# Two column chunks in step: each weight pass of a tile run for one chunk, then the other, in two PSUM banks

## The chip, the cores and the metric

The kernel runs on one core of one Trainium2 chip. The metric is the device time of one execution in microseconds (us), as the median of several runs. A profiled execution of the same kernel gives the trace from which the rows below are read.

## The reference

Two small transformer blocks follow each other on one sequence of 512 tokens, width 1024, in float32. The first puts 16 meta tokens ahead (528 tokens in all) and has two layers: differential attention and a gated MLP with a causal convolution of width 3, then latent attention and the same MLP again. The second has a projection, a convolution branch and a windowed attention branch, gates, and a third MLP. Cut to what matters here:

```python
def conv_ffn(h, g_norm, w_in, conv_w, conv_b, w_out):
    xn = rms_norm(h, g_norm)
    a, b = jnp.split(xn @ w_in, 2, axis=-1)            # 1024 -> 2 x 2816
    ap = jnp.pad(a, ((0, 0), (CONV_W - 1, 0), (0, 0)))
    a_conv = conv_b
    for j in range(CONV_W):
        a_conv = a_conv + ap[:, j:j + L] * conv_w[j]
    return h + (jax.nn.silu(a_conv) * b) @ w_out       # 2816 -> 1024

h = concatenate([meta, x])                             # 528 tokens
h = diff_attn_layer(h, ...);  h = conv_ffn(h, ...)     # layer 0
k_nope, k_rope, v = shared_latent_kv(h, ...)
h = mla_layer(h, ...);        h = conv_ffn(h, ...)     # layer 1
x = rms_norm(h, final_norm)[:, 16:]                    # 512 tokens
return second_block(x, ...)
```

## The kernel before

Tokens lie along the free dimension and features along the 128 partitions, so an activation of width 1024 is 8 blocks of 128 rows. The weights come from HBM as one stream of "halves" of 128 x 1024 values (8 blocks of 128 x 128) through a ring of four buffers. ScalarE rounds a half to `w_hi` (fp32r, the form that TensorE multiplies in one pass), GpSimd writes the remainder to `w_lo`. Activations are held as such pairs too: `x_hi`, `x_lo` and `g_hi`, `g_lo`. A product of full precision is then three passes per block, hi x hi, hi x lo and lo x hi (`passes`, lines 789, 790, 791 of the kernel, in this order: `x_hi` with `w_hi`, `x_lo` with `w_hi`, `x_hi` with `w_lo`).

An output tile is 128 features by T tokens, and `tile` computes it on TensorE from one half of weights, with 8 blocks (6 in the last down projection of a layer's MLP). T is T1 = 528, T3 = 516 or T2 = 512. A PSUM bank holds 512 float32 columns, so `chunks(T)` gives one chunk for T2 and two chunks of T/2 columns for T1 (264) and T3 (258), in banks 2(j mod 2) and 2(j mod 2) + 1. Before the change a tile of two chunks runs all blocks for the first chunk, then all blocks for the second: 24 passes in one bank, 24 in the next. The next tile uses the other two banks. VectorE is released by `half_done` after the last pass of the tile, reads both banks in one instruction, and gives them back by `tile_taken`.

Within a tile, TensorE waits once for the weights (`lo_ready`) and for the bank pair (`tile_taken`), and before each block for the activation (`ready`, which is `x_ready` or `g_ready`). That last wait only stands in the first chunk.

Which two-chunk tiles go through `tile`, by the calls in the program: tiles 2 to 7 of the output projection of layer 0 (T1), the 44 up tiles of the first MLP (T1) and tiles 2 to 7 of its last down projection (T1, 6 blocks), three tiles of the query latent (T1), tiles 2 to 7 of the output projection of layer 1 (T3), and the 22 tiles at even places among the up tiles of the second MLP (T3; those at odd places are T2, one chunk). Tiles of one chunk, the paired first two tiles of a projection (`tile_pair`), the attention pieces and the down projections in `product` do not pass through the edited lines.

Of the kernel before, what the change touches and what calls it, by code (L numbers as in the profile page):

```python
# [32 lines left out]
P = 128  # L33
# [109 lines left out]
def ring(j):  # L143

    return (j + 2 * len([d for d in DOWNS.values() if d.j < j])) % 4
# [101 lines left out]
def program(nc, x_t, stream, params, positions, out):  # L247
    tabs_dram = nc.inline_tensor(rotary_tables(), "rotary_tables").ap()
    consts_dram = nc.inline_tensor(shape_constants(), "shape_constants").ap()
    with ExitStack() as ctx:  # L250
# [8 lines left out]
        w_hi = sb("w_hi", [P, 4, HW], F32R)  # L259
        w_lo = sb("w_lo", [P, 4, HW], F32R)  # L260
# [138 lines left out]
        ps = ctx.enter_context(nc.psum_tensor("ps", [P, 8, 512], F32))  # L399
# [141 lines left out]
        def chunks(T):  # L541

            return [(0, 0, T2)] if T == T2 else [(0, 0, T // 2), (1, T // 2, T // 2)]
# [241 lines left out]
        def _(pe):  # L785
            def passes(out_ap, j, b, xh, xl, k, cols, first, last):

                s, c = ring(j), slice(b * P, (b + 1) * P)
                nc.tensor.matmul(out_ap, w_hi[:, s, c], xh[:, k, cols], start=first, stop=False)  # L789
                nc.tensor.matmul(out_ap, w_hi[:, s, c], xl[:, k, cols], start=False, stop=False)  # L790
                return nc.tensor.matmul(out_ap, w_lo[:, s, c], xh[:, k, cols], start=False, stop=last)  # L791

            def tile(j, tl, blocks, xh, xl, T, ready, i=0, first=0):

                pe.wait_ge(lo_ready, j + 1 + 4 * i)
                wait(pe, tile_taken, tl - 1 - int(after_down(j)) + 4 * i)
                for bank, t0, n in chunks(T):
                    for b in range(blocks):
                        if ready and not bank:
                            pe.wait_ge(ready[0], ready[1] + b + 1)  # L800
                        last = passes(ps[:, 2 * (j % 2) + bank, 0:n], j, b, xh, xl, b,
                                      slice(first + t0, first + t0 + n), b == 0, b == blocks - 1)
                last.then_inc(half_done, 1)

            def pair_blocks(j, tl, m, n, blocks, xh, xl, T, ready, b0=0, b1=KD):
# [539 lines left out]
            for m in range(TILES_C):  # L1345
# [4 lines left out]
                if m == 3:  # L1350
                    pe.wait_ge(y_ready, 2)
                    for b in range(4):
                        last = nc.tensor.transpose(ps[:, 3, b * P:b * P + P], vt2[:, b * P:b * P + P], ident)
                    last.then_inc(vt2_done, 1)
                for u in range(8):
                    g, n = divmod(u, 4)
                    s_at = unit2_at(u)
                    k0 = 0 if n else P
                    if m == s_at + 2:
                        pe.wait_ge(p2_ready, u + 1)  # L1360
                        wait(pe, pt2_ready, u)
                        for i in range(4):
                            for kb in range(k0 // P, 2):
                                last = nc.tensor.transpose(ps[:, 6 + kb, i * P:i * P + P],
                                                           prob2[:, i, kb * P:kb * P + P], ident)
# [12 lines left out]
                for u in range(8):  # L1378
                    g, n = divmod(u, 4)
# [1439 lines left out]
```

## Time and profile before

| | |
|---|---|
| runs | 2045.72, 2044.54, 2044.59 us; median 2044.59 us |
| the profiled execution | 2045.36 us, span 2043.6 us |
| TensorE busy | 2020.7 us of the span, 13376 matmuls and as many weight loads |
| VectorE, ScalarE, GpSimd busy | 1322.9, 853.1, 1160.5 us |
| granted TensorE clock | mean 0.999 |
| bytes over DMA | 183.06 MB, mean 90 GB/s |

The busy time of TensorE counts the records of matmuls that overlap: a record lasts from the start of a pass to its modelled end, and the next pass starts well before that. The pace of the engine is therefore read from start to start.

### The profile page before, as it was taken

To read this page: it belongs to the slowest core of one execution; us is meant where nothing else is said; L and a number is where in the kernel's file an instruction comes from. 1 tells how busy PE (TensorE), PEld (TensorE's weight loads), DVE (VectorE), ACT (ScalarE), POOL (GpSimd) and SP (SyncE) were. 2 spreads that over 40 slices of the span, in tenths; PEclk is the share of its full clock that TensorE was granted. 3 is DMA by queue.
4 is the path that set the end of the run, shared out by engine and by line. 5 is a ranking of instruction groups with operands and counts; after the bars stand their busy time and mean duration, and the time that the engine had idled before them with its cause. 6 is when DMAs were issued, how large, how long until landed. Compare 5 with 4: busy or idle time off the path is not lost.

```text
span 2043.6 us, 37435 instructions
## 1 busy us (share of the span) xinstructions
PE 2020.7 (99%) x13376; PEld 1806.5 (88%) x13376; DVE 1322.9 (65%) x2193; ACT 853.1 (42%) x1493; POOL 1160.5 (57%) x1395
## 2 busy tenths in 40 slices
PE   9999999999999999999999999999999999999998
PEld 8889899999999988899998998777788888888987
DVE  7777757847746868856857768865512457857654
ACT  5444534432433477724432425344422234433433
POOL 6444356666657522146675767744445557666755
PEclk9999999999999999999999999999999999999999
DMA  5222122232233301122233233322223223232322
GB/s 188 75 73 81 53 83 93 78 114 89 88 108 104 104 32 43 32 89 93 71 118 100 87 99 103 112 80 78 82 93 99 87 83 102 84 113 83 124 83 83
DMA packets 51986, 183.06 MB, mean 90 GB/s; under 512 B 5648, under 2 KB 7824, under 8 KB 51856
## 3 DMA queue, kind: packets, MB, share of 16 engines
q1 hardware_dynamic: 50304, 178.87, 27.1%
q10 hardware_dynamic: 1552, 2.42, 0.3%
q8 instruction: 87, 1.43, 0.3%
q14 instruction: 43, 0.35, 0.1%
HBM read 179.17 MB, written 2.10 MB: 89 GB/s over the span
## 4 chain that ended last, share of the span: by engine, by line
PE 97%; DVE 2%; issue 1%; ACT 1%; DVEq 0%; ACTq 0%
PE ps L789 25%; PE ps L790 24%; PE ps L791 24%; PE ps L913 4%; PE ps L914 4%; PE ps L915 4%; PE ps L1162 2%; PE ps L1179 1%; PE ps L1072 1%; PE ps L1172 1%; PE ps L1103 1%; PE ps L1087 1%; PE ps L861 1%; PE ps L1173 0%; PE ps L1105 0%
## 5 line engine op out<-in xcount | busy, mean ns | idle before, releaser
L723 POOL TENSOR_TENSOR w_lo<-w_raw,w_hi 128x256 fp32r<-128x256 f32 x1140 | 962.6, 879 | 762.8 <-ACT w_hi L2219 742.0
L789 PE MATMUL ps<-x_hi,w_hi 128*128 128x264 f32 (+2 forms) x2504 | 823.1, 329 | 0.1
L790 PE MATMUL ps<-x_lo,w_hi 128*128 128x264 f32 (+2 forms) x2504 | 813.6, 325 | 0.0
L791 PE MATMUL ps<-x_hi,w_lo 128*128 128x264 f32 (+2 forms) x2504 | 812.3, 324 | 0.0
L789 PEld LDWEIGHTS ps<-x_hi,w_hi 128*128 128x128 f32 x2504 | 471.3, 188 | 49.9 <-issue 5.4
L790 PEld LDWEIGHTS ps<-x_lo,w_hi 128*128 128x128 f32 x2504 | 470.8, 188 | 42.1 <-issue 0.2
L791 PEld LDWEIGHTS ps<-x_hi,w_lo 128*128 128x128 f32 x2504 | 471.3, 188 | 39.6
L2219 ACT ACTIVATE w_hi<-w_raw 128x1024 fp32r<-128x1024 f32 x267 | 278.1, 1049 | 67.1 <-PE ps L791 51.4
L789 PE MATMUL ps<-g_hi,w_hi 128*128 128x264 f32 (+3 forms) x648 | 207.9, 321 | 1.0 <-DVE g_lo L1878 1.0
L790 PE MATMUL ps<-g_lo,w_hi 128*128 128x264 f32 (+3 forms) x648 | 205.9, 318 | 0.0
L791 PE MATMUL ps<-g_hi,w_lo 128*128 128x264 f32 (+3 forms) x648 | 205.6, 317 | 0.0
L2354 ACT ACTIVATE scratch<-scratch,par 128x512 f32<-128x512 f32 (+1 forms) x66 | 54.2, 821 | 342.3 <-DVE scratch L1603 342.3
L743 POOL TENSOR_TENSOR w_lo<-w_raw,w_hi 128x256 fp32r<-128x256 f32 x144 | 125.8, 902 | 75.6 <-ACT w_hi L2236 75.3
L789 PEld LDWEIGHTS ps<-g_hi,w_hi 128*128 128x128 f32 x648 | 121.9, 188 | 11.7 <-DVE g_lo L1878 1.4
L790 PEld LDWEIGHTS ps<-g_lo,w_hi 128*128 128x128 f32 x648 | 122.0, 188 | 9.2
L791 PEld LDWEIGHTS ps<-g_hi,w_lo 128*128 128x128 f32 x648 | 122.1, 188 | 8.7
L2153 DVE TENSOR_TENSOR scratch<-ps,acc 128x512 f32<-128x512 f32 x46 | 31.8, 691 | 120.3 <-PE ps L791 120.2
L914 PE MATMUL ps<-g_lo,w_hi 128*128 128x256 f32 (+1 forms) x384 | 108.4, 282 | 0.0
L915 PE MATMUL ps<-g_hi,w_lo 128*128 128x256 f32 (+1 forms) x384 | 108.0, 281 | 0.0
L913 PE MATMUL ps<-g_hi,w_hi 128*128 128x256 f32 (+1 forms) x384 | 107.9, 281 | 0.0
L1609 DVE SCALAR_TENSOR_TENSOR scratch<-scratch,par 128x512 f32<-128x512 f32 (+1 forms) x66 | 53.9, 817 | 71.3 <-ACT scratch L2354 71.3
L1617 DVE TENSOR_TENSOR scratch<-ps,r 128x512 f32<-128x512 f32 (+1 forms) x66 | 46.0, 696 | 77.6 <-PE ps L791 77.5
(278 smaller groups left out, 3052.8 us busy)
## 6 DMA issues: line engine op xcount, KB each, us to landing
w_raw<-stream SPq DMA_DIRECT2D x334, 512.0 KB, 3.5
h<-x_t SPq DMA_DIRECT2D x4, 528.0 KB, 6.9
out_t<-h SPq DMA_DIRECT2D x6, 256.0 KB, 2.3
scratch<-rotary_tables ACTq DMA_DIRECT2D x4, 264.0 KB, 5.3
out_t<-h ACTq DMA_DIRECT2D x2, 256.0 KB, 2.5
par<-params ACTq DMA_DIRECT2D x1, 342.0 KB, 4.9
scratch<-positions ACTq DMA_DIRECT2D x1, 256.0 KB, 2.6
cst<-shape_constants ACTq DMA_DIRECT2D x1, 193.0 KB, 6.0
```

What stands on the lines that cost most here:

```text
L723: last = nc.gpsimd.tensor_tensor(w_lo[:, ring(j), cols], w_raw[:, j % 4, cols], w_hi[:, ring(j), cols].bitcast(F32), ALU.subtract)
L743: last = nc.gpsimd.tensor_tensor(chunks_lo[:, slot, cols], src[:, cols], chunks_hi[:, slot, cols].bitcast(F32), ALU.subtract)
L789: nc.tensor.matmul(out_ap, w_hi[:, s, c], xh[:, k, cols], start=first, stop=False)
L790: nc.tensor.matmul(out_ap, w_hi[:, s, c], xl[:, k, cols], start=False, stop=False)
L791: return nc.tensor.matmul(out_ap, w_lo[:, s, c], xh[:, k, cols], start=False, stop=last)
L913: nc.tensor.matmul(out_ap, wh, xh, start=opens and q == 0, stop=False, skip_group_check=True)
L914: nc.tensor.matmul(out_ap, wh, xl, start=False, stop=False, skip_group_check=True)
L915: last = nc.tensor.matmul(out_ap, wl, xh, start=False, stop=q == 3, skip_group_check=True)
L1609: V.scalar_tensor_tensor(conv[:, 0:Tn], a_pad[:, c0 + 1:c0 + 1 + Tn], tap(1), conv[:, 0:Tn], ALU.mult, ALU.add).then_inc(conv_step, 1)
L1617: V.tensor_tensor(cut(b_val[:, 0:Tn], Tn), result(j + 1, Tn), cut(r[:, c0:T], Tn), ALU.mult).then_inc(tile_taken, 1)
L2219: A.activation(w_hi[:, ring(j), :], w_raw[:, j % 4, :], ACT.Copy).then_inc(hi_ready, 1)
L2354: A.activation(conv[:, 0:Tn], a_pad[:, T - Tn:T], ACT.Identity, bias=par[:, bass.ds(b + 2 * i, 1)], scale=par[:, bass.ds(o + 2 * i, 1)]).t ...
```

## The change

The loop over the chunks moves inward. For each block the three passes (weights, activation) are taken in the old order, and each is run for the first chunk in the one bank, and then for the second chunk in the other. The wait for a block's activation stands ahead of its first pass.

```diff
                 wait(pe, tile_taken, tl - 1 - int(after_down(j)) + 4 * i)
-                for bank, t0, n in chunks(T):
-                    for b in range(blocks):
-                        if ready and not bank:
-                            pe.wait_ge(ready[0], ready[1] + b + 1)
-                        last = passes(ps[:, 2 * (j % 2) + bank, 0:n], j, b, xh, xl, b,
-                                      slice(first + t0, first + t0 + n), b == 0, b == blocks - 1)
+                s = ring(j)
+                for b in range(blocks):
+                    if ready:
+                        pe.wait_ge(ready[0], ready[1] + b + 1)
+                    hi, lo = [w[:, s, b * P:b * P + P] for w in (w_hi, w_lo)]
+                    for w, x in ((hi, xh), (hi, xl), (lo, xh)):
+                        for bank, t0, n in chunks(T):
+                            last = nc.tensor.matmul(ps[:, 2 * (j % 2) + bank, 0:n], w,
+                                                    x[:, b, first + t0:first + t0 + n],
+                                                    start=b == 0 and w is hi and x is xh,
+                                                    stop=b == blocks - 1 and w is lo)
                 last.then_inc(half_done, 1)
```

The instructions of TensorE at the start of the first MLP's second up tile (the loop's first), before. `ps` is PSUM, without the bank; the registers are those of the loop's waits:

```order
L244 REGISTER_ALU [waits lo_ready]
L789 MATMUL ps<-x_hi,w_hi 128x264 [waits x_ready,tile_taken]
L790 MATMUL ps<-x_lo,w_hi 128x264
L791 MATMUL ps<-x_hi,w_lo 128x264
L789 MATMUL ps<-x_hi,w_hi 128x264 [waits x_ready]
L790 MATMUL ps<-x_lo,w_hi 128x264
L791 MATMUL ps<-x_hi,w_lo 128x264
```

And at the same place in the changed kernel:

```order
L244 REGISTER_ALU [waits lo_ready]
L804 MATMUL ps<-x_hi,w_hi 128x264 [waits x_ready,tile_taken]
L804 MATMUL ps<-x_hi,w_hi 128x264
L804 MATMUL ps<-x_lo,w_hi 128x264 x2
L804 MATMUL ps<-x_hi,w_lo 128x264 x2
L804 MATMUL ps<-x_hi,w_hi 128x264 [waits x_ready]
L804 MATMUL ps<-x_hi,w_hi 128x264
L804 MATMUL ps<-x_lo,w_hi 128x264 x2
L804 MATMUL ps<-x_hi,w_lo 128x264 x2
```

The passes of the second chunk, which stood 24 places later, now stand behind those of the first. Each weight block is named by two instructions (`w_lo`) or four (`w_hi`) in a row, and six passes instead of three lie between two waits for `x_ready`. In the second MLP, where a tile of one chunk ends and one of two chunks begins, the changed kernel has:

```order
L804 MATMUL ps<-x_hi,w_lo 128x512
L795 REGISTER_ALU
L244 REGISTER_ALU [waits lo_ready]
L804 MATMUL ps<-x_hi,w_hi 128x258 [waits x_ready,tile_taken]
L804 MATMUL ps<-x_hi,w_hi 128x258
L804 MATMUL ps<-x_lo,w_hi 128x258 x2
L804 MATMUL ps<-x_hi,w_lo 128x258 x2
```

The one-chunk tiles keep their order. The number of matmuls is the same in both kernels, and the other engines have the same instructions in the same order.

## Rows read from the trace of the kernel before

**Rows 1.** The page: busy time of TensorE, and the chain that ended last.

```profile
PE 2020.7 (99%) x13376; PEld 1806.5 (88%) x13376; DVE 1322.9 (65%) x2193; ACT 853.1 (42%) x1493; POOL 1160.5 (57%) x1395
...
PE 97%; DVE 2%; issue 1%; ACT 1%; DVEq 0%; ACTq 0%
PE ps L789 25%; PE ps L790 24%; PE ps L791 24%; PE ps L913 4%; PE ps L914 4%; PE ps L915 4%; PE ps L1162 2%; PE ps L1179 1%; PE ps L1072 1%; PE ps L1172 1%; PE ps L1103 1%; PE ps L1087 1%; PE ps L861 1%; PE ps L1173 0%; PE ps L1105 0%
```

**Rows 2.** Stretches of both MLPs: length, then PE, PEld, DVE, ACT, POOL, PEclk, DMA.

```profile
297.00:680.00 383.00, 380.61 (x3119) 379.77 (x3118) 252.24 (x320) 145.53 (x198) 249.81 (x292) 1.00 0.30 96
...
914.00:1283.00 369.00, 366.37 (x2409) 334.54 (x2408) 264.73 (x335) 150.26 (x208) 250.24 (x287) 1.00 0.30 97
```

**Rows 3.** Timeline (start us, length us): first and last passes of three up stretches.

```profile
301.08 0.28 PE L789 MATMUL ps<-x_hi,w_hi 128*128 128x264 f32 x1
...
388.68 0.28 PE L791 MATMUL ps<-x_hi,w_lo 128*128 128x264 f32 x1
...
431.32 0.28 PE L789 MATMUL ps<-x_hi,w_hi 128*128 128x264 f32 x1
...
524.75 0.28 PE L791 MATMUL ps<-x_hi,w_lo 128*128 128x264 f32 x1
...
567.43 0.28 PE L789 MATMUL ps<-x_hi,w_hi 128*128 128x264 f32 x1
...
637.47 0.28 PE L791 MATMUL ps<-x_hi,w_lo 128*128 128x264 f32 x1
```

**Rows 4.** Timeline: starts of three tiles in a row of the second MLP.

```profile
923.72 0.28 PE L789 MATMUL ps<-x_hi,w_hi 128*128 128x258 f32 x1
...
929.46 0.39 PE L789 MATMUL ps<-x_hi,w_hi 128*128 128x512 f32 x1
...
935.02 0.28 PE L789 MATMUL ps<-x_hi,w_hi 128*128 128x258 f32 x1
```

**Rows 5.** Groups of TensorE by shape: count, busy us, mean ns, idle before.

```profile
L789 PE MATMUL ps<-x_hi,w_hi 128*128 128x264 f32 x1224 | 357.1, 292 | 0.1
...
L789 PE MATMUL ps<-x_hi,w_hi 128*128 128x258 f32 x352 | 99.4, 282 | 0.0
...
L789 PE MATMUL ps<-g_hi,w_hi 128*128 128x264 f32 x272 | 78.4, 288 | 1.0 <-DVE g_lo L1878 1.0
...
L789 PE MATMUL ps<-g_hi,w_hi 128*128 128x258 f32 x128 | 37.1, 290 | 0.0
```

**Rows 6.** Timeline: two passes of `first_keys`, which changes the bank every third pass.

```profile
17.62 0.28 PE L790 MATMUL ps<-x_lo,w_hi 128*128 128x264 f32 x1
...
20.52 0.28 PE L790 MATMUL ps<-x_lo,w_hi 128*128 128x264 f32 x1
```

**Rows 7.** Timeline: `sum_of_parts`, four passes on the same weights `ones`.

```profile
300.58 0.28 PE L871 MATMUL ps<-g_hi,ones 128*128 128x264 f32 x1
300.59 0.19 PEld L872 LDWEIGHTS ps<-g_lo,ones 128*128 128x128 f32 x1
300.70 0.29 PE L872 MATMUL ps<-g_lo,ones 128*128 128x264 f32 x1
...
300.83 0.28 PE L871 MATMUL ps<-g_hi,ones 128*128 128x264 f32 x1
...
300.95 0.29 PE L872 MATMUL ps<-g_lo,ones 128*128 128x264 f32 x1
```

**Rows 8.** Timeline: the last block's first pass in each MLP's first tile.

```profile
297.01 0.28 PE L791 MATMUL ps<-x_hi,w_lo 128*128 128x264 f32 x1
297.20 0.39 PE L789 MATMUL ps<-x_hi,w_hi 128*128 128x264 f32 x1
297.43 0.28 PE L790 MATMUL ps<-x_lo,w_hi 128*128 128x264 f32 x1
...
914.10 0.28 PE L791 MATMUL ps<-x_hi,w_lo 128*128 128x258 f32 x1
914.33 0.40 PE L789 MATMUL ps<-x_hi,w_hi 128*128 128x258 f32 x1
```

## The prediction

> **What bounds the kernel now.** I read the page first. TensorE is busy for 99% of the span, and 97% of the chain that ended last is its own matmuls; the three lines of `passes` alone are 73% of it [rows 1]. The reader should not take busy time for pace, since the records overlap. So I went on to the stretches of the two MLPs: TensorE stands idle for 2.4 us of 383 in the first and 2.6 us of 369 in the second, and the granted clock is 1.00, which is the 2.4 GHz level, in both [rows 2]. No transfer, no eviction and no rounding of weights sets the end there. What a pass costs from its own start to the next one's is therefore the quantity that the change can move, and little else.
>
> The pace comes from the timeline. Three stretches of up tiles in the first MLP run without a stall: 720, 768 and 576 passes of 264 columns, of which the last starts 87.60, 93.43 and 70.04 us after the first [rows 3]. Divided by 719, 767 and 575 steps that is 121.8 ns for each. In the second MLP a tile of 48 passes of 258 columns takes 929.46 - 923.72 = 5.74 us, 119.6 ns a pass, and the tile of 24 passes of 512 columns behind it 5.56 us, 231.7 ns a pass [rows 4]. From these two, a column costs (231.7 - 119.6) / 254 = 0.441 ns, and a pass has 119.6 - 258 x 0.441 = 5.8 ns that do not depend on its columns. An estimate from two shapes, but it tells how much a hand-over between passes can give back at all.
>
> **How many passes are touched.** By the calls listed with the kernel: at 264 columns 6 x 48 (output projection) + 44 x 48 (up) + 6 x 36 (last down) + 3 x 48 (query latent) = 2760; at 258 columns 6 x 48 + 22 x 48 = 1344. Together 4104, which fits under the counts by shape of each of the three lines, where attention pieces and paired tiles take the rest [rows 5]. Their time is 2760 x 121.8 ns + 1344 x 119.6 ns = 336 + 161 = 497 us, a quarter of the span. One nanosecond on each is 4.1 us, 0.2%.
>
> **The change part by part.** It removes and adds no matmul, weight load, wait or transfer. Three things move.
>
> 1. The bank changes after every pass instead of every 24. A tile of 48 passes has 47 steps within it, one of them a change of bank before and all of them after: 46 more, 34 more in a tile of 36. With 81 and 6 such tiles, 3726 + 204 = 3930 steps become bank changes. What one costs is in the trace already. In the stretches of [rows 3] I sorted the 2061 steps. Those from a first chunk to a first chunk take 120.9 ns on the mean (989 of them), from second to second 122.8 ns (989), from first to second, with a change of bank, 123.0 ns (43, standard error 0.7), and from second to the next tile's first, also with a change of bank, 120.0 ns (40). A step is as long as the chunk that it leads to makes it, whichever bank it comes from. After the change half of the steps lead to either chunk: (123.0 + 120.0) / 2 = 121.5 ns in place of (120.9 + 122.8) / 2 = 121.85, or 0.3 ns less. Times 3930 that is -1.3 us. The start of the kernel says the same at a denser rate: `first_keys` changes the bank after every third pass, and 24 of its steps take 20.52 - 17.62 = 2.90 us, 120.8 ns each [rows 6]. Clocks of 10 ns resolution don't carry more than that, so the bounds are taken wider below.
>
> 2. The same weights are named by consecutive matmuls. Before, one step in three keeps its weights (from line 789 to 790); after, four in six. Within the same stretches [rows 3] the steps from 789 to 790, which keep the weights, take 121.9 ns, those from 790 to 791 121.7 and those from 791 to the next 789 121.9, with 685 to 688 of each. Keeping the weights gains nothing. The loads are still made: four passes in a row on `ones` have their own weight load and follow each other after 0.12, 0.13 and 0.12 us [rows 7]. I take 0. The bounds: at most the 5.8 ns that hang on the pass and not on the columns; on the other side, nothing in the sorted steps shows a loss above 0.3 ns.
>
> 3. The wait for a block's activation. Six passes instead of three lie between two such waits, so TensorE asks for the last block of the first tile later by seven blocks of 0.36 us. In the first MLP that block makes it wait: its first pass starts 0.19 us after the one ahead of it, and the second 0.23 us after that, since its weight load was held back too; 0.12 would be usual for both. In the second MLP the first of these steps is 0.23 us [rows 8]. That is 0.07 + 0.11 us in the one, and the same way about 0.2 us in the other: -0.4 us together. No wait is added, and at its place in the tile nothing is queued behind it that wasn't before. VectorE is released by the tile's last pass in both orders, so its work, and the weight ring behind `half_done`, keep their times.
>
> Sum: -1.3 + 0 - 0.4 = -1.7 us. The profiled execution took 2045.36 us with a span of 2043.6, 0.8 us above the median of the runs, 2044.59; the steps are alike in both, so I take the sum from the median: **2042.9 us**. That is 0.08% and within 0.2% of before, about what a measurement of this kernel can tell from no change (4.1 us). The case's own range is 2040.5 to 2046, from -0.9 to +0.45 ns a pass.
>
> **The rivals.**
>
> A. The hand-over gets shorter. Either the second pass of a pair finds its weights in place, or it no longer follows its predecessor into the same bank, where that one's record is still open (a record is 0.28 us, a step 0.12). If every second pass loses the 5.8 ns, 2052 x 5.8 = 11.9 us go, and the time is 2044.6 - 11.9 - 0.4 = 2032.3 us; if every pass loses them, 23.8 us and 2020.4 us. For it speaks that no step of the trace has both, kept weights and a new bank. Against it, each of the two alone shows nothing [rows 3, 6, 7]. It decides from 0.9 ns a pass.
> The Trainium skill, "TensorE: Matmul & The Clock Gate", under "Step-by-step: what each phase is for", says that loads and matmuls are split so that weights can be loaded once and used for many matmuls; by that rule this order would save a load for each pair. The trace has a load for each pass, on the same weights too.
>
> B. Slower: each bank change costs. The 43 steps from first to second chunk stand 0.3 ns above their kind, with a standard error of 0.7; two errors up that is 1.7 ns, and if the return costs the same, 3930 x 1.7 = 6.7 us, 2044.6 + 6.7 - 0.4 = 2050.9 us. It decides from 1.1 ns a change. Against it stand the 40 returns, all 120.0, and the 120.8 ns at the start.
>
> C. Slower by far: the clock. If changing banks let the granted clock fall to 1.2 GHz, the 497 us would take up to twice as long: some 2540 us. Against it, the clock is 1.00 where banks change every 24 passes, and the engine has no pause that the new order would lengthen [rows 2].
> The Trainium skill, same page, under "A second HAM failure mode: psum-queue depth-cycling", reports a kernel that cycled through banks and in which the clock swung between its levels. That rule speaks against this change; there the engine idled between groups, here no row shows such a pause.
>
> **How the numbers follow.** The forecast has 0.58, A 0.25, B 0.15, C 0.02. The price of A between 1 and 5.8 ns on half of the passes is open, so the range reaches to its nearer end, 2032, and to B's 2051: left out are A's far half, C and the tails, under 2 in 10. Faster by over 0.2% is A, slower B and C.
>
> **What would show it.** In the changed kernel the three up stretches should again have 121.8 ns a step, and steps to the second chunk be about 1.5 to 3 ns longer than those to the first, now alternating. TensorE and its weight loads should keep 13376 records each, the clock 1.00, and the gap at the last block of each first MLP tile be gone. I am wrong if the pace of the two-chunk tiles shifts by over 1 ns, which would be seen at once as 0.1 us or more on every 5.85 us tile, while the tiles of 512 columns keep 231.7 ns.

## The result, and the profile after

The changed kernel takes 2047.9 us (median, 2047.12 to 2048.47) against 2045.1 us (2044.41 to 2045.72) for the kernel before on the same chip: a ratio of 1.0013, with a 95% interval of 1.0008 to 1.0019. It is 2.8 us slower. That is under the prediction's bound of 0.2% and within its whole range, 2032 to 2051 us, but above the range of the forecast itself, 2040.5 to 2046 us, and the sign is not the one that the sum gave.

The page of the changed kernel, busy time and chain, as in [rows 1]:

```profile
PE 2022.4 (99%) x13376; PEld 1807.7 (88%) x13376; DVE 1320.3 (65%) x2193; ACT 853.2 (42%) x1493; POOL 1160.0 (57%) x1395
...
PE 96%; DVE 2%; issue 1%; ACT 1%; DMA 0%; POOL 0%; DVEq 0%; SPq 0%; ACTq 0%
PE ps L804 59%; PE ps L789 5%; PE ps L791 5%; PE ps L790 5%; PE ps L918 4%; PE ps L919 4%; PE ps L920 4%; PE ps L1167 2%; PE ps L1184 1%; PE ps L1077 1%; PE ps L1177 1%; PE ps L1108 1%; PE ps L1092 1%; PE ps L866 1%; PE ps L1178 0%
```

Its windows over the two MLPs, with the columns of [rows 2]:

```profile
297.00:680.00 383.00, 380.65 (x3112) 379.93 (x3111) 250.72 (x318) 145.13 (x197) 249.95 (x292) 1.00 0.30 96
914.00:1283.00 369.00, 366.34 (x2405) 334.82 (x2405) 262.46 (x335) 149.65 (x209) 247.29 (x285) 1.00 0.29 96
```

Next to nothing that a page counts has moved: as many matmuls and weight loads, 96% of the chain in place of 97%, the clock at 1.00 and no new idle time. What is left is the pace, from start to start. The timeline of the changed kernel, where an "x2" is one row for the passes of both chunks:

```profile
299.08 0.41 PE L804 MATMUL ps<-x_hi,w_lo 128*128 128x264 f32 x2
299.33 0.40 PE L804 MATMUL ps<-x_hi,w_hi 128*128 128x264 f32 x2
299.57 0.41 PE L804 MATMUL ps<-x_lo,w_hi 128*128 128x264 f32 x2
...
431.11 0.41 PE L804 MATMUL ps<-x_hi,w_hi 128*128 128x264 f32 x2
...
525.06 0.29 PE L918 MATMUL ps<-g_hi,w_hi 128*128 128x264 f32 x1
...
924.35 0.40 PE L804 MATMUL ps<-x_hi,w_hi 128*128 128x258 f32 x2
...
930.15 0.40 PE L804 MATMUL ps<-x_hi,w_hi 128*128 128x512 f32 x1
...
935.74 0.28 PE L804 MATMUL ps<-x_hi,w_hi 128*128 128x258 f32 x1
...
1045.73 0.40 PE L804 MATMUL ps<-x_hi,w_hi 128*128 128x258 f32 x2
...
1136.82 0.28 PE L918 MATMUL ps<-g_hi,w_hi 128*128 128x256 f32 x1
```

The timeline of the kernel before at the ends of the same two stretches, whose first start at 431.32 stands in [rows 3], and of one more in the third MLP, which the change does not touch:

```profile
524.87 0.28 PE L913 MATMUL ps<-g_hi,w_hi 128*128 128x264 f32 x1
...
1044.52 0.28 PE L789 MATMUL ps<-x_hi,w_hi 128*128 128x258 f32 x1
...
1134.97 0.28 PE L913 MATMUL ps<-g_hi,w_hi 128*128 128x256 f32 x1
...
1802.67 0.39 PE L789 MATMUL ps<-x_hi,w_hi 128*128 128x512 f32 x1
...
1891.64 0.28 PE L913 MATMUL ps<-g_hi,w_hi 128*128 128x256 f32 x1
```

Two stretches serve as rulers from here on. **Stretch A** is the second group of up tiles in the first MLP, 768 passes of 264 columns: 524.87 - 431.32 = 93.55 us before (121.8 ns a pass) and 525.06 - 431.11 = 93.95 us after (122.3 ns). **Stretch B** is the second group in the second MLP, 8 tiles of 258 columns and 8 of 512 in turn: 90.45 us before and 91.09 us after. Both are read from one start to another within one execution, and kernels that should have the same pace agree in them within 0.01 us (`e1_in_step`, `e5b_one_bank` and `e8_weights_hi` below). The medians of whole runs, by their intervals, tell kernels apart only from 1 to 2 us on. Where steps are given below to 0.1 ns, they are means over the starts as the trace holds them, to 1 ns; the rows shown are rounded to 10 ns.

In [rows 4] a tile of 258 columns takes 5.74 us, and here 930.15 - 924.35 = 5.80 us. The tile of 512 columns behind it takes 5.59 us in place of 5.56 (5.593 and 5.565 us on the mean), though its own passes and their order are as before.

If the whole of each trace is laid beside the other at instructions that are no part of a tile, the changed kernel is 0.38 us ahead at 29 us (the first loads, which vary by half a microsecond from run to run), 0.52 us ahead at 300 us, 0.46 us behind at 680 us, 0.63 us at 918 us, 2.29 us at 1284 us and 2.31 us at 2036 us. All of it is lost where two-chunk tiles run, nothing in the second block.

### The profile page after: what moved, and what is told of

Its sections match the earlier page's. It is cut to its first block, busy times and chain, and to the rows that moved or that the text cites. A ratio compares the mean times of both kernels' runs of the same rounds, so it can differ in the third digit from the quotient of the medians.

```text
span 2045.9 us, 37435 instructions
## 1 busy us (share of the span) xinstructions
PE 2022.4 (99%) x13376; PEld 1807.7 (88%) x13376; DVE 1320.3 (65%) x2193; ACT 853.2 (42%) x1493; POOL 1160.0 (57%) x1395
## 4 chain that ended last, share of the span: by engine, by line
PE 96%; DVE 2%; issue 1%; ACT 1%; DMA 0%; POOL 0%; DVEq 0%; SPq 0%; ACTq 0%
PE ps L804 59%; PE ps L789 5%; PE ps L791 5%; PE ps L790 5%; PE ps L918 4%; PE ps L919 4%; PE ps L920 4%; PE ps L1167 2%; PE ps L1184 1%; PE ps L1077 1%; PE ps L1177 1%; PE ps L1108 1%; PE ps L1092 1%; PE ps L866 1%; PE ps L1178 0%
## 5 line engine op out<-in xcount | busy, mean ns | idle before, releaser
L804 PE MATMUL ps<-x_hi,w_hi 128*128 128x512 f32 (+2 forms) x1952 | 569.2, 335 | 0.0
L804 PE MATMUL ps<-x_lo,w_hi 128*128 128x512 f32 (+2 forms) x1952 | 568.9, 335 | 0.0
L804 PE MATMUL ps<-x_hi,w_lo 128*128 128x512 f32 (+2 forms) x1952 | 567.3, 335 | 0.0
L804 PEld LDWEIGHTS ps<-x_hi,w_lo 128*128 128x128 f32 x1952 | 332.6, 189 | 38.8
L789 PE MATMUL ps<-x_hi,w_hi 128*128 128x264 f32 (+1 forms) x552 | 169.3, 307 | 0.8 <-POOL w_lo L754 0.7
L791 PE MATMUL ps<-x_hi,w_lo 128*128 128x264 f32 (+1 forms) x552 | 160.4, 291 | 0.0
L790 PE MATMUL ps<-x_lo,w_hi 128*128 128x264 f32 (+1 forms) x552 | 160.2, 290 | 0.0
L804 PE MATMUL ps<-g_hi,w_hi 128*128 128x264 f32 (+2 forms) x456 | 120.2, 319 | 0.0
L804 PE MATMUL ps<-g_lo,w_hi 128*128 128x264 f32 (+2 forms) x456 | 120.2, 319 | 0.0
L804 PE MATMUL ps<-g_hi,w_lo 128*128 128x264 f32 (+2 forms) x456 | 120.0, 319 | 0.0
```

Of the source, the lines that this page charges most:

```text
L804: last = nc.tensor.matmul(ps[:, 2 * (j % 2) + bank, 0:n], w, x[:, b, first + t0:first + t0 + n], start=b == 0 and w is hi and x is xh, sto ...
```

## The experiments

All of them edit the loop in `tile` alone, up to the last two. They give the two chunks lines of their own and take the six passes of a block from a list of (weights, activation, chunk), where 0 is hi or the first chunk and 1 is lo or the second:

```python
for b in range(blocks):
    if ready:
        pe.wait_ge(ready[0], ready[1] + b + 1)
    for n_pass, (w, x, c) in enumerate(order):
        bank, t0, n = parts_of[c]
        run = second_chunk if c else first_chunk
        last = run(ps[:, 2 * (j % 2) + bank, 0:n], (w_hi, w_lo)[w][:, s, b * P:b * P + P],
                   (xh, xl)[x][:, b, first + t0:first + t0 + n], ...)
```

All results together; ratios are to the kernel before on the same chip, with their 95% interval:

| kernel | us | ratio | A, us | B, us |
|---|---|---|---|---|
| before | 2044.6 to 2045.2 | 1 | 93.55 | 90.45 |
| after | 2047.9 | 1.0013 (1.0008 to 1.0019) | 93.95 | 91.09 |
| e1_in_step | 2047.9 | 1.0014 (1.0005 to 1.0024) | 93.95 | 91.09 |
| e2_banks_only | 2046.5 | 1.0009 (0.9999 to 1.0018) | 93.95 | 90.61 |
| e3_every_third | 2042.7 | 0.9988 (0.9979 to 0.9998) | 92.80 | 90.61 |
| e4_snake | 2045.5 | 1.0001 (0.9992 to 1.0011) | 93.01 | 91.11 |
| e5b_one_bank | 2047.9 | 1.0014 (1.0003 to 1.0026) | 93.95 | 91.10 |
| e6_same_columns | 2044.6 | 0.9999 (0.9988 to 1.0010) | 93.21 | 90.94 |
| e7_before_same_columns | 2043.5 | 0.9994 (0.9983 to 1.0006) | 93.00 | 90.61 |
| e8_weights_hi | 2047.7 | 1.0014 (1.0002 to 1.0025) | 93.95 | 91.10 |
| e10_in_step_256 | 2048.7 | 1.0018 (1.0008 to 1.0028) | 94.29 | 90.88 |
| e11_before_256 | 2043.7 | 0.9993 (0.9983 to 1.0002) | 93.02 | 90.61 |
| e12_third_at_264 | 2042.5 | 0.9987 (0.9978 to 0.9997) | 92.81 | 90.45 |
| e13_sixth_at_264 | 2044.6 | 0.9998 (0.9989 to 1.0006) | 93.44 | 90.46 |
| e14_in_step_weights_0 | 2047.9 | 1.0013 (1.0001 to 1.0024) | 93.95 | 91.09 |
| e15_before_weights_0 | 2045.2 | 1.0000 (0.9989 to 1.0011) | 93.54 | 90.45 |
| e16_in_step_x_0 | 2027.4 | 0.9914 (0.9886 to 0.9943) | 92.16 | 90.34 |
| e17_before_x_0 | 2031.3 | 0.9933 (0.9910 to 0.9955) | 92.96 | 90.50 |
| e18_before_rows_2304 | 2032.9 | 0.9940 (0.9927 to 0.9954) | 92.96 | 90.44 |
| e19_in_step_rows_2304 | 2030.2 | 0.9928 (0.9914 to 0.9941) | 92.16 | 90.34 |

### Bank, weights, or the order as such

**The change again, with a line for each chunk**, so that steps can be told apart:

```diff
+order = [(0, 0, 0), (0, 0, 1), (0, 1, 0), (0, 1, 1), (1, 0, 0), (1, 0, 1)]
```

> The changed kernel's order, written so that the passes of the first and the second chunk stand on lines of their own. Every theory: the time of the changed kernel, 2.7 us over the one before, with the up tiles of the first MLP 0.5 ns a pass and those of 258 columns 1.2 to 1.7 ns a pass above the kernel before. The new lines should show which of the steps (first to second chunk, second to first) is longer than 122.8 and 120.9 ns.

The timeline of this kernel, one block of stretch A:

```profile
431.98 0.28 PE L798 MATMUL ps<-x_hi,w_hi 128*128 128x264 f32 x1
432.11 0.28 PE L801 MATMUL ps<-x_hi,w_hi 128*128 128x264 f32 x1
432.23 0.28 PE L798 MATMUL ps<-x_lo,w_hi 128*128 128x264 f32 x1
432.35 0.28 PE L801 MATMUL ps<-x_lo,w_hi 128*128 128x264 f32 x1
432.47 0.28 PE L798 MATMUL ps<-x_hi,w_lo 128*128 128x264 f32 x1
432.59 0.28 PE L801 MATMUL ps<-x_hi,w_lo 128*128 128x264 f32 x1
...
525.93 0.29 PE L925 MATMUL ps<-g_hi,w_hi 128*128 128x264 f32 x1
```

Stretch A is 525.93 - 431.98 = 93.95 us, as in the changed kernel. A single step in these rows is too coarse to say anything; over all blocks of the stretch the six steps take 122.4, 121.1, 124.1, 121.6, 121.9 and 122.9 ns. Each leads to a bank other than the one before it. Those that keep the weights (first, second, third and fifth) take 122.4, 121.1, 124.1 and 121.9, those that change them 121.6 and 122.9: neither property sorts them.

**The bank at every pass, but other weights at five steps of six, and the other activation array at four of six** (in the changed kernel two and two):

```diff
-order = [(0, 0, 0), (0, 0, 1), (0, 1, 0), (0, 1, 1), (1, 0, 0), (1, 0, 1)]
+order = [(0, 0, 0), (1, 0, 1), (0, 1, 0), (0, 0, 1), (1, 0, 0), (0, 1, 1)]
```

> The chunk and so the bank alternates with every pass, but the weights change between five of six passes (hi, lo, hi, hi, lo, hi), less often kept than before. Theory P (a change of bank costs): as slow as the changed kernel, +2.7 us against the one before. Theory W (loading a weight block again right behind itself costs): no slower than the kernel before, 0 to -1 us. Theory M (the second chunk's columns read right behind the first's cost): +1 to +2.7 us, as four of six steps no longer go from a chunk to its neighbour in the same array.

Stretch A is the same to 0.01 us, and the six steps have the same times by their position in the block. Stretch B gives back 0.48 of the 0.64 us. So at 264 columns it isn't the naming of equal weights that costs. At 258 columns weights and arrays changed together here; since `e8_weights_hi` below leaves B at 91.10 us, it is the order of the arrays that counts.

**Three passes of a block in one bank, then three in the other:**

```diff
+order = [(0, 0, 0), (0, 1, 0), (1, 0, 0), (0, 0, 1), (0, 1, 1), (1, 0, 1)]
```

> Per block the three passes of the first chunk, then the three of the second: the wait for the activation moves as in the change, the weights are kept as often as before, the bank changes every third pass. Theory P: a third of the loss, about +0.6 us after the 0.4 us that the wait gives back. Theory W: -0.4 us. Theory M: +0.6 us or less.

The timeline at the ends of both stretches:

```profile
429.94 0.28 PE L798 MATMUL ps<-x_hi,w_hi 128*128 128x264 f32 x1
...
522.74 0.28 PE L925 MATMUL ps<-g_hi,w_hi 128*128 128x264 f32 x1
...
1041.66 0.28 PE L798 MATMUL ps<-x_hi,w_hi 128*128 128x258 f32 x1
...
1132.27 0.28 PE L925 MATMUL ps<-g_hi,w_hi 128*128 128x256 f32 x1
```

522.74 - 429.94 = 92.80 us, 0.75 us less than before. An order that changes banks eight times as often as the old one is faster than it, which no price on a change of bank can give.

**The chunk order turned at the second activation**, so that the bank stays for one step in three:

```diff
+order = [(0, 0, 0), (0, 0, 1), (0, 1, 1), (0, 1, 0), (1, 0, 0), (1, 0, 1)]
```

> The changed kernel with the second activation's two chunks swapped: first, second, second, first, first, second. The weights are kept four times in six as in the change, the bank changes on three or four steps of six instead of all. Theory P: half to two thirds of the loss, +1.3 to +1.8 us. Theory W: all of it, +2.7 us. Theory M: between them, two of three neighbours in order remain.

A gains 0.54 us on the old order, and B loses 0.66. For this order the gain turns into a loss between 264 and 258 columns.

**The changed order with both chunks in the first chunk's bank and columns:**

```diff
-ps[:, 2 * (j % 2) + bank, 0:n]
+ps[:, 2 * (j % 2) + 0, 0:n]
```

> The changed order, but the passes of both chunks are written into the first chunk's bank and columns, so no bank changes inside a tile (the output is not the reference's: the second chunk's sums are added to the first's, and its own bank keeps old values). Theory P (the bank change costs): the loss goes, steps of 264 columns back at 121.8 ns and of 258 at 119.6 ns, the total at the kernel before or 0.4 us under it. Theory M (only where the columns are read matters): as the changed kernel, 122.3 and 120.7 ns, +2.7 us.

Its timeline:

```profile
431.25 0.28 PE L798 MATMUL ps<-x_hi,w_hi 128*128 128x264 f32 x1
...
525.20 0.29 PE L925 MATMUL ps<-g_hi,w_hi 128*128 128x264 f32 x1
```

525.20 - 431.25 = 93.95 us, with no change of bank within a tile, as with one at each pass. The bank costs nothing and gives nothing. The prediction's first term and its rivals A and B all stood on it.

**The changed order with the rounded weights in all passes**, so that one block of weights is named six times in a row:

```diff
-(w_hi, w_lo)[w][:, s, b * P:b * P + P]
+(w_hi, w_hi)[w][:, s, b * P:b * P + P]
```

> The changed order with w_hi in all three passes, so five of six steps keep their weights and w_lo is never read in these tiles (the output is not the reference's). Theory W (loading the same block again right behind itself costs): slower than the changed kernel, by a quarter of its loss, 0.7 us or more. Otherwise: as the changed kernel, within 0.5 us, unless the addresses of the weights matter by themselves.

93.95 us again, to the hundredth.

### Where the passes read

With bank and weights gone, what a pass reads from the activations is left: which block, which array and which columns.

**The changed order, the second chunk reading the first chunk's columns:**

```diff
-(xh, xl)[x][:, b, first + t0:first + t0 + n]
+(xh, xl)[x][:, b, first + 0:first + 0 + n]
```

> The changed order with both banks, but the second chunk reads the activation columns of the first again (the output is not the reference's). Theory M: the alternation of addresses is gone, every step becomes one between equal addresses, near the 120.9 ns that first chunks had at 264 columns, and the total falls 2 us or more under the kernel before. Theory P: the loss of the bank changes stays, so the steps of 264 columns remain 0.5 ns or more above those of a kernel without the change of bank that reads the same columns.

**The old order with the same reads:**

```diff
-x[:, b, first + t0:first + t0 + n]
+x[:, b, first + 0:first + 0 + n]
```

> The order of the kernel before, with the second chunk reading the first's columns (the output is not the reference's). It is the partner of the run above. If the 1.9 ns between second and first chunks come from where the second one's columns begin, all steps here are 120.9 ns at 264 columns and the total is about 2.6 us under the kernel before; if they come from the bank that is written, they stay at 120.9 and 122.8. Theory P: this kernel is faster than the same reads in step; theory M: the two are equal.

Both get faster in A than their order was, by 0.74 and 0.55 us. In the old order the steps within a first and within a second chunk, 120.9 and 122.8 ns in the prediction, now take the same time, so the difference lay in the columns at which a chunk begins, and not in the bank it writes. In the changed order the blocks show what is left: six passes take 723 ns in two blocks of each four, and 733 ns in the other two. `x_hi` has rows of 528 values, 2112 bytes, which is 8 x 256 + 64. So from block to block the row begins 64 bytes further in a unit of 256, and after four blocks at the same place. The third MLP shows the same period in the kernel before: in the 16 tiles of 512 columns that begin at 1802.67, the passes of blocks 0 to 3 take 230.0, 232.7, 232.3 and 231.7 ns on the mean, and those of blocks 4 to 7 the same again.

**The second chunk at a whole number of 256-byte units behind the first** (column 256, which leaves 8 columns read twice and the last 8 unread), in either order:

```diff
-first + t0:first + t0 + n
+first + (0, 256)[c]:first + (0, 256)[c] + n
```

> The changed order, with the second chunk reading from column 256 on, so that it begins 1024 bytes behind the first instead of 1056 or 1032 (it reads 8 or 2 columns twice; the output is not the reference's). Theory M by alignment of the chunk's first column: the loss goes, the steps equal those of the partner run within 0.2 ns. Theory M by the order in which the activation is read, whatever the alignment: the order still costs about 0.2 to 1 ns a step against the partner run, as it did when both chunks read the same columns.

> The order of the kernel before, with the second chunk read from column 256 on (the output is not the reference's). Theory M by alignment: all steps of 264 columns at 120.9 to 121.4 ns, as with the same columns for both, and those of 258 at 119.6 to 119.9. If the second chunk's 122.8 ns stay, its first column's alignment was not their cause.

The old order gains 0.53 us in A, as much as by equal columns. The changed order loses 0.34 us more there (and gains 0.21 us in B). The place of the second chunk matters, but setting it alone does not make the changed order a good one.

**Chunk by chunk in each block at 264 columns, the old order at 258**, and then with the chunks' order turned in every other block:

```diff
+steps = [(c, b) for b in range(blocks) for c in (0, 1)]
```

> Tiles of 264-column chunks take per block three passes of the first chunk, then three of the second; tiles of 258-column chunks keep the order of the kernel before. By the stretches of the run with every third pass, 1.0 ns a pass is gained on 2760 passes, and the 0.4 ns a pass that its 258-column tiles lost is not paid: -2.8 to -3.1 us, 0.9985 of the kernel before. If the gain there came from the wait alone, -0.4 us.

```diff
-steps = [(c, b) for b in range(blocks) for c in (0, 1)]
+steps = [(c, b) for b in range(blocks) for c in ((0, 1), (1, 0))[b % 2]]
```

> As the run beside it, with the chunks' order turned on every other block, so that the chunk changes every sixth pass. If the step from one chunk to the other is what gains (120.0 to 120.8 ns in the run with every third pass, against 121.8 on the mean), half of that gain goes: -1.7 us. If the rate only depends on how far apart equal rows are read, it stays near -2.8 us.

The first repeats the gain of `e3_every_third` at 264 columns (92.81 us) and leaves B at 90.45 us. The second gives most of it up (93.44 us), though it changes banks half as often. The steps inside a chunk's three passes, which both kernels have, take 121.0 ns on the mean in the first and 121.3 ns in the second, and the step from one chunk to the other within a block 121.0 and 123.3 ns. So a step has no fixed price by its kind.

**One block of weights throughout**, in both orders, as a check on the side of the weights' addresses:

```diff
-(w_hi, w_lo)[w][:, s, b * P:b * P + P]
+(w_hi, w_lo)[w][:, s, 0:P]
```

> The changed order, every block multiplied with the first block of its weight half, so that the weight address stands still over a tile but for high and low part (the output is not the reference's). If the loss hangs on the activation's addresses alone, steps as in the changed kernel, 122.3 ns at 264 columns and 120.7 at 258, 0.5 and 1.1 above the partner run. If it hangs on where a block of weights is loaded from while a chunk streams, the two partners come together.

> The order of the kernel before with the same standing weight address (the output is not the reference's). Activation alone: 121.8 and 119.6 ns as in the kernel before. Weights: another pace, equal to that of the partner run.

Both keep the times of their order within 0.01 us in A. Which block of a half's weights is loaded doesn't matter.

**One block of activations throughout**, in both orders. All passes of a tile read rows that begin at the same place:

```diff
-(xh, xl)[x][:, b, first + t0:first + t0 + n]
+(xh, xl)[x][:, 0, first + t0:first + t0 + n]
```

> The changed order with the activation's first block read for every block of weights (the output is not the reference's). Its rows lie 2112 bytes apart, so the blocks begin at other addresses; here only chunk and array still alternate. If the loss comes from chunk and array alternating, it stays against the partner run: 0.5 ns at 264 columns, 1.1 at 258. If it comes from the walk over the blocks' addresses, it goes or turns.

> The order of the kernel before with the activation's first block read for every block of weights (the output is not the reference's). Partner of the run above. If the walk over blocks matters at all, the pace leaves 121.8 and 119.6 ns here.

The timeline of stretch A in the changed order on block 0:

```profile
428.35 0.28 PE L798 MATMUL ps<-x_hi,w_hi 128*128 128x264 f32 x1
...
520.51 0.28 PE L925 MATMUL ps<-g_hi,w_hi 128*128 128x264 f32 x1
```

And in the old order:

```profile
429.59 0.28 PE L798 MATMUL ps<-x_hi,w_hi 128*128 128x264 f32 x1
...
522.55 0.28 PE L922 MATMUL ps<-g_hi,w_hi 128*128 128x264 f32 x1
```

92.16 us is 120.0 ns a pass, and 92.96 us 121.0. Both kernels are 14 to 18 us faster than before, and the order of the two is turned: on one block the passes in step are the faster ones. Most of the gain lies in the tiles of 512 columns, which these two kernels run on block 0 too: 227 ns a pass in the third MLP in place of 231.7. The tiles of 512 columns in the second MLP, also on block 0, gain next to nothing: 231.5 to 231.7 ns. Stretch B hardly moves for that reason.

### The whole computation on rows that begin alike

If the place where rows begin is the cause, the real computation must gain as much when each row of `x_hi` and `x_lo` starts at a multiple of 256 bytes from the others. The last two kernels lay hi and lo rows in turn, 576 values (2304 bytes, 9 x 256) apart, and leave nothing out. Room comes from `acc`, which moves into the last row's tail (in the part not shown, `small` and `scratch` shrink a little and `sq` is allocated earlier):

```diff
-x_hi = sb("x_hi", [P, KD, T1], F32R)
-x_lo = sb("x_lo", [P, KD, T1], F32R)
+xs = sb("xs", [P, (2 * KD - 1) * ROW + 2 * T1])
+x_rows = nc.alloc_sbuf_tensor_at("x_rows", [P, KD, 2, ROW], F32R, offset=xs_at)
+x_hi, x_lo = x_rows[:, :, 0, 0:T1], x_rows[:, :, 1, 0:T1]
...
-acc = sb("acc", [P, T1])
+acc = xs[:, (2 * KD - 1) * ROW + T1:(2 * KD - 1) * ROW + 2 * T1]
```

In the old order:

> The order of the kernel before, with the rows of x_hi and x_lo laid 2304 bytes apart in memory instead of 2112 (576 columns of room for 528), high and low part of a block in neighbouring rows, so that every block begins at the same offset within 256 bytes. Nothing of the computation is left out. Theory (the pace of a pass follows where the activation rows of consecutive passes begin): the 2256 passes of 512 columns in the second block's projection, attention output and MLP go from 231.7 to 227.2 ns, as they did when one block was read throughout, -10.2 us; the 2112 of 264 columns in the first MLP from 121.8 to 121.1, -1.5 us; in sum 2033 us, with the attention's pieces open. Rival (the pace there came from reading the same block again and again): no change, 2045 us.

In the changed order:

> The same rows 2304 bytes apart with the changed order. If the loss of the change comes from how its order walks over rows that begin at four different offsets, it turns into a gain here: 264-column steps of the first MLP at 120.0 ns against 121.1 in the run beside it, those of 258 columns 0.6 ns below, so 2.5 to 3 us faster than that run, about 2030 us. If the loss belongs to the order whatever the rows, it stays 2.8 us slower than that run.

The timeline of the old order on these rows, with the ends of stretch A, of the output projection of layer 1 and of the third MLP's group (`x_rows` holds both parts):

```profile
430.50 0.28 PE L801 MATMUL ps<-x_rows,w_hi 128*128 128x264 f32 x1
...
523.46 0.28 PE L925 MATMUL ps<-g_hi,w_hi 128*128 128x264 f32 x1
...
875.23 0.28 PE L801 MATMUL ps<-g_hi,w_hi 128*128 128x258 f32 x1
...
909.69 0.40 PE L801 MATMUL ps<-x_rows,w_hi 128*128 128x258 f32 x2
...
1793.52 0.63 PE L801 MATMUL ps<-x_rows,w_hi 128*128 128x512 f32 x2
...
1880.60 0.28 PE L925 MATMUL ps<-g_hi,w_hi 128*128 128x256 f32 x1
```

The timeline of the changed order on them, the first pass of stretch A and five in a row from its third and fourth block, the ends of A and B, a tile of 512 columns within B, and ahead of it the output projection of layer 1:

```profile
428.94 0.28 PE L801 MATMUL ps<-x_rows,w_hi 128*128 128x264 f32 x1
...
430.74 0.28 PE L804 MATMUL ps<-x_rows,w_hi 128*128 128x264 f32 x1
430.86 0.28 PE L801 MATMUL ps<-x_rows,w_lo 128*128 128x264 f32 x1
430.98 0.28 PE L804 MATMUL ps<-x_rows,w_lo 128*128 128x264 f32 x1
431.10 0.28 PE L801 MATMUL ps<-x_rows,w_hi 128*128 128x264 f32 x1
431.22 0.28 PE L804 MATMUL ps<-x_rows,w_hi 128*128 128x264 f32 x1
...
521.10 0.28 PE L928 MATMUL ps<-g_hi,w_hi 128*128 128x264 f32 x1
...
872.25 0.28 PE L801 MATMUL ps<-g_hi,w_hi 128*128 128x258 f32 x1
...
907.05 0.28 PE L801 MATMUL ps<-x_rows,w_hi 128*128 128x258 f32 x1
...
1039.53 0.28 PE L801 MATMUL ps<-x_rows,w_hi 128*128 128x258 f32 x1
...
1045.26 0.63 PE L801 MATMUL ps<-x_rows,w_hi 128*128 128x512 f32 x2
...
1050.82 0.28 PE L801 MATMUL ps<-x_rows,w_hi 128*128 128x258 f32 x1
...
1129.87 0.28 PE L928 MATMUL ps<-g_hi,w_hi 128*128 128x256 f32 x1
```

Stretch A is 92.96 us in the old order and 521.10 - 428.94 = 92.16 us in the changed one, each equal to its kernel on block 0, and in the latter 766 of the 768 steps take 120 ns and the other two 121 and 122 ns. The 384 passes of 512 columns in the third MLP take 1880.60 - 1793.52 = 87.08 us, 226.8 ns each, where they took 1891.64 - 1802.67 = 88.97 us, 231.7 ns. The whole kernel takes 2032.9 us (0.9940) in the old order and 2030.2 us (0.9928) in the changed one. The changed order costs 2.8 us on the old rows and gains 2.7 us on the new ones, and with them it is the fastest kernel of the study that computes the whole result, 14.9 us below the one before. Both expectations on record, 2033 and about 2030 us, came.

These two kernels also hold their own control. The six tiles of the output projection of layer 1 read `g_hi` and `g_lo`, whose rows are still 2112 bytes apart. Their 288 passes of 258 columns take 909.69 - 875.23 = 34.46 us in the old order and 907.05 - 872.25 = 34.80 us in the changed one, a loss of 1.2 ns a pass. In stretch B of the same kernels, on the new rows, the tiles of 258 columns take 119.7 ns a pass in the old order and 119.4 in the changed one. So the new order loses in these tiles, whose rows drift, and gains in those whose rows begin alike, in the same two executions; the new places of other buffers don't explain that. Rows that drift do not always make it lose, though: in the last down projection of the first MLP, tiles of six blocks of `g` instead of eight, its 216 passes of 264 columns take 121.5 ns in place of 121.85, on the old rows as in these two kernels.

Not every pass on these rows gains, though. In the second MLP a tile of 512 columns begins at column 4 of its rows, 16 bytes in (`first` is T3 - T2), and it takes 1050.82 - 1045.26 = 5.56 us, 231.7 ns a pass, as on the old rows. Its rows lie as those of the third MLP do, which are read from column 0 on at 226.8 ns. The pace is the same in the first and the last twelve passes of the tile, so the tile of 258 columns ahead of it does not explain it. In the old order, too, the steps within a first chunk of stretch A take 120.4 ns on the mean and those within a second, which begins 1056 bytes (4 x 256 + 32) further in, 121.6 ns. So it is not the distance between rows alone that sets the pace, but also where in 256 bytes a pass itself begins.

## Why the prediction was wrong in sign

**Term 1, the bank at every pass: this is the step that failed.** The sum gave -1.3 us for it, from the sentence "A step is as long as the chunk that it leads to makes it, whichever bank it comes from". That the bank itself costs nothing is right (`e5b_one_bank` and `e1_in_step` have the same 93.95 us), but what followed from it was not. The 120.9 and 122.8 ns were no property of the chunk: they came from where its columns begin, beside where those of the pass ahead began (`e7_before_same_columns` makes the two equal). The 43 steps from first to second chunk and the 40 back are also always the same ones, from the last block to the first. They say nothing of a step from one chunk to the other in the same block, of which the new order has five in each block. There the steps to the second chunk take 122.4, 124.1 and 121.9 ns and those to the first 121.1, 121.6 and, on to the next block, 122.9. Their mean is 122.3 ns in place of 121.5, and to the second chunk they are 0.9 ns longer than to the first, not 1.5 to 3 ns.

The 123.0 and 120.0 ns of the term were also coarse: they were sorted from starts rounded to 10 ns. From the starts to 1 ns the 43 steps take 122.5 and the 40 returns 120.8 ns, each with a standard error under 0.1 ns. The term would then have been some -0.8 us, with the same sign, so the rounding is not what failed.

Sized by what was measured, the term is 2760 x 0.52 ns = 1.4 us at 264 columns, 1344 x 1.1 ns = 1.5 us at 258, and a part that the prediction did not have at all: 22 tiles of 512 columns behind an in-step tile, 28 ns longer each, 0.6 us. Together some +3.5 us, an estimate, since A and B stand for all tiles. It is somewhat high: the two traces shift by 2.7 us between 29 us and 2036 us. Read directly, the three long groups of up tiles in the first MLP lose 0.35, 0.40 and 0.30 us and those in the second 0.57, 0.64 and 0.48 us. That is 2.7 us in all, so that the remaining two-chunk tiles and the waits come out even between them: the output projection of layer 1 loses 1.2 ns on each of 288 passes, and the last down projection gains 0.35 ns on each of 216.

**Term 2, weights named again: right, 0.** 13376 loads before and after, and no gain from four or six passes on the same block (`e8_weights_hi`, `e14_in_step_weights_0`).

**Term 3, the wait for a block's activation: right in kind.** In [rows 8] the last block's first pass is held back twice, by 0.07 and 0.11 us. In the changed kernel the pairs there start at 299.08, 299.33 and 299.57, 0.25 and 0.24 us apart: the gap is gone. At the next instruction that is no part of a tile, `sum_of_parts` at 300 us, the changed kernel had gained 0.19 us over its mark at 240 us, although 336 passes in the new order lie between (six tiles of the output projection and the first up tile). The same place in the second MLP can't be read apart from them.

**The rivals.** A fell with the bank and with the weights. B gave a loss, as measured, but for a reason that doesn't hold; its price of 1.7 ns came from the standard error of 0.7 ns, which starts to 1 ns bring under 0.1 ns. C did not come: the granted clock stayed at 0.999 with a bank change at each of the 4104 passes, with 0.999 in the kernel before. The Trainium skill, "TensorE: Matmul & The Clock Gate", under "A second HAM failure mode: psum-queue depth-cycling", speaks of cycling through banks; here TensorE has no pause between the passes, and the row shows no swing.

**The sign of being wrong** that the prediction gave was a shift of over 1 ns a pass while tiles of 512 columns keep 231.7 ns. At 264 columns the shift is 0.5 ns, at 258 it is 1.1 ns, and the tiles of 512 columns behind the latter did not keep theirs (233.1 ns). The sign was also set too high: over 48 passes 1 ns makes 0.05 us a tile, not 0.1 us, and the whole result is only 0.7 ns on each of the 4104 passes.

**What is shown, and what isn't.** Shown: bank, weight block and repeated naming of weights leave the pace as it is; reading one block, or rows at multiples of 256 bytes, takes 2.0 to 2.1% off a pass of 512 columns that begins at column 0, nothing off one that begins at column 4, 0.6% off one of 264 in the old order and 1.9% in the changed one, and turns the order of the two kernels round. So what the change moved was the walk over rows that begin at four different places in 256 bytes; on rows that begin alike the same new order gains. The loss belongs to tiles of eight blocks on such rows: those of six blocks gained. Argued only: what in the memory or in its path makes such a walk slow, and why one order on the old rows is better (`e3_every_third`) and another worse; no run gives a rule by which an order's time could be worked out ahead. Multiples of 64 bytes are not enough, since 2112 is 33 x 64. Left open: whether multiples of 128 bytes would do as well as 256, which start columns other than 0 are fast (4 is not, in tiles of 512 columns), what of the gain comes from hi and lo rows lying in turn rather than from their distance (the same pace on one block, where they don't, speaks for the distance), and what other rows for `g_hi` and `g_lo`, which kept their layout for want of room, would give.

## What to carry to other kernels

When TensorE streams without a stall, there can be 1 to 2% left in its pace that hangs on where in 256 bytes consecutive passes begin to read the activation. Lay these rows at a multiple of 256 bytes from each other first, see which passes start at the row's beginning (here only those of 512 columns that did gained the 2%), and order the passes afterwards, because an order tuned on rows that drift by 64 bytes can turn from loss to gain when they are set right. And a sample of steps from one trace prices a new order only if it has the same pairs of passes in it; 83 steps that were all the same seam did not.

## What the runs showed of the hardware

- The pace of back-to-back matmuls in fp32r depends on where the moving rows begin. 512 columns from column 0 on: 231.7 ns on rows 2112 bytes apart, 230.0 to 232.7 ns by block with a period of four blocks, and 226.8 ns on rows 2304 bytes apart. 512 columns from column 4 on, 16 bytes in: 231.7 ns on the latter rows too (`e19_in_step_rows_2304`). 264 columns in tiles of eight blocks: 120.8 to 122.8 ns on the former, by order and by where the second chunk begins (`e3_every_third`, `e10_in_step_256`), 121.0 and 120.0 ns on rows 2304 bytes apart. The Trainium skill, "SBUF — State Buffer", under "Specifications (TRN2)", gives lines of 16 bytes. All rows here begin on a multiple of 16 bytes of each other, 2112 being 132 x 16, so that line alone does not tell the two layouts apart.
- The effect reaches over a tile's edge: a tile of 512 columns took 5.593 us behind an in-step tile of 258 columns and 5.565 us behind the old one, with its own passes unchanged. On rows 2304 bytes apart the tile takes 5.560 us behind either.
- A weight block named in 2, 4 or 6 passes in a row, or one block of `w_hi` and one of `w_lo` through a whole tile, changes nothing in the pace of an order (A stays at 93.95 us in the changed one), and neither does a change of PSUM bank at each pass (93.95 us with and without it).
